# Folding the input product of a Fourier mixing layer on VectorE, with its gates opened first

## The reference

```
F_GROUPS, F_GROUP_DIM = 8, 128

def fourier_mix(u):
    ug = u.astype(jnp.float32).reshape(B, S, F_GROUPS, F_GROUP_DIM)
    y = jnp.fft.fft2(ug, axes=(1, 3), norm='ortho').real
    return y.reshape(B, S, F_WIDTH).astype(u.dtype)

def token_mix(h, w_in, w_fourier, w_ret, w_out):
    proj = h @ w_in
    u_f, q, k, v, g, a_f, a_r = jnp.split(proj, offsets, axis=-1)
    y_f = fourier_mix(u_f) @ w_fourier
    y_r = retention_branch(q, k, v, g) @ w_ret
    merged = jax.nn.sigmoid(a_f) * y_f + jax.nn.sigmoid(a_r) * y_r
    return merged @ w_out

h = rmsnorm_2(x, norm1_g[l]) * (1.0 + sc1) + sh1
x = x + g1 * token_mix(h, ...)
```

## Time and profile before

| | us |
|---|---|
| median of 3 runs | 2947.02 |
| lowest, highest | 2945.31, 2947.09 |
| the profiled execution, own time | 2945.48 |
| its span, first to last instruction | 2943.6 |

### The profile page before, as it was taken

How to read it: one execution, slowest core, us unless ns; L and a number is a source line. 1 busy time by engine, 2 the same in 40 slices (tenths; PEclk the granted TensorE clock), 3 DMA queues, 4 the chain that set the end, 5 groups by cost and what they waited for, 6 DMA issues and landing times.

```text
span 2943.6 us, 49397 instructions
## 1 busy us (share of the span) xinstructions
PE 2927.3 (99%) x19714; PEld 2451.0 (83%) x19714; DVE 1533.1 (52%) x2181; ACT 1105.5 (38%) x1663; POOL 1559.3 (53%) x1910
## 2 busy tenths in 40 slices
PE   9999999999999999999999999999999999999998
PEld 7877777788888888988888898888988888888887
DVE  5467787424556666753334274435542432473635
ACT  4454434333443332443433243323433342342323
POOL 6432233356546676546444556565465445575654
PEclk9999999999999999999999999999999999999999
DMA  5211111233326777423222223232233222223232
GB/s 172 92 45 41 42 54 57 93 143 101 122 97 221 253 273 252 148 79 128 85 92 72 93 87 115 86 107 85 94 108 115 78 77 94 93 94 99 95 100 72
DMA packets 92005, 320.50 MB, mean 109 GB/s; under 512 B 10112, under 2 KB 14336, under 8 KB 91520
## 3 DMA queue, kind: packets, MB, share of 16 engines
q1 hardware_dynamic: 84256, 301.34, 30.8%
q10 hardware_dynamic: 7520, 15.99, 1.6%
HBM read 313.36 MB, written 3.93 MB: 108 GB/s over the span
## 4 chain that ended last, share of the span: by engine, by line
PE 97%; issue 1%; POOL 1%; DMA 0%; DVE 0%; ACT 0%; SPq 0%; POOLq 0%; ACTq 0%; DVEq 0%
PE bank L826 26%; PE bank L830 25%; PE bank L827 25%; PE bank L1152 2%; PE bank L819 2%; PE bank L1163 2%; PE bank L820 2%; PE bank L821 2%; PE bank L1171 1%; POOL w_lo L757 1%; PE bank L858 1%; PE bank L857 1%; PE bank L856 1%; PE bank L1678 1%; PE bank L1677 1%
## 5 line engine op out<-in xcount | busy, mean ns | idle before, releaser
L757 POOL TENSOR_TENSOR w_lo<-w_raw,w_hi 128x256 fp32r<-128x256 f32 x1800 | 1464.8, 847 | 1044.5 <-ACT w_hi L1750 1034.5
L826 PE MATMUL bank<-act,w_hi 128*128 128x512 f32 (+1 forms) x3592 | 1363.0, 379 | 2.1 <-POOL w_lo L757 1.5
L830 PE MATMUL bank<-act,w_lo 128*128 128x512 f32 (+1 forms) x3592 | 1342.0, 374 | 0.0
L827 PE MATMUL bank<-act,w_hi 128*128 128x512 f32 (+1 forms) x3592 | 1340.9, 373 | 0.0
L826 PEld LDWEIGHTS bank<-act,w_hi 128*128 128x128 f32 x3592 | 676.7, 188 | 128.1 <-issue 9.3
L830 PEld LDWEIGHTS bank<-act,w_lo 128*128 128x128 f32 x3592 | 676.4, 188 | 120.5
L827 PEld LDWEIGHTS bank<-act,w_hi 128*128 128x128 f32 x3592 | 677.1, 189 | 111.0
L1750 ACT CAST w_hi<-w_raw 128x1024 fp32r<-128x1024 f32 x452 | 471.3, 1049 | 340.5 <-DMA w_raw<-in_weights 160.7
L1758 ACT ACTIVATE arena<-bank 128x512 f32<-128x512 f32 (+1 forms) x177 | 104.4, 594 | 416.5 <-PE bank L830 399.9
L775 POOL TENSOR_TENSOR stats<-stats,exponent 128x8 f32<-128x8 f32 (+2 forms) x38 | 46.6, 1226 | 299.5 <-DVE stats L2742 150.0
L2428 DVE TENSOR_TENSOR act<-tmp,act 128x512 fp32r<-128x512 f32 (+1 forms) x140 | 122.1, 872 | 77.6 <-ACT act L1777 72.7
(11 more groups left out here) (327 smaller groups left out, 2814.0 us busy)
## 6 DMA issues: line engine op xcount, KB each, us to landing
w_raw<-in_weights SPq DMA_DIRECT2D x469, 512.0 KB, 3.4
arena<-in_ada SPq DMA_DIRECT2D x96, 512.0 KB, 4.8
arena<-in_strips ACTq DMA_DIRECT2D x8, 448.0 KB, 3.6
arena<-in_x ACTq DMA_DIRECT2D x1, 2048.0 KB, 10.4
y_scratch<-tmp ACTq DMA_DIRECT2D x7, 256.0 KB, 2.0
arena<-y_scratch ACTq DMA_DIRECT2D x1, 1792.0 KB, 7.9
arena<-in_x SPq DMA_DIRECT2D x3, 512.0 KB, 7.8
arena<-in_lora_w ACTq DMA_DIRECT2D x8, 128.0 KB, 2.2
```

The lines of the kernel that those rows point to most:

```text
L757: ins = nc.gpsimd.tensor_tensor(w_lo[:, k, cols], weights_of(u)[:, cols], w_hi[:, k, cols].bitcast(F32), ALU.subtract)
L826: nc.tensor.matmul(o, wh, xh, start=first, stop=False)
L827: nc.tensor.matmul(o, wh, xl, start=False, stop=False)
L830: mm = nc.tensor.matmul(o, wl, xh, start=False, stop=last)
```

## The change

It replaces step 2 and reorders step 3 in both layers.

- **The order.** The first three tiles, those of the opening, are now gate tiles, and gates 3 and 4 follow. Then come nine folded tiles (`folded_tile`): a middle one with 8 output rows, and an even and an odd one for each of four pairs of feature groups, each 24 matmuls of 258 or 256 columns. Gates 5, 6 and 7 and the transforms stand between them as the list `FOURIER_ORDER` says. The eight output tiles come behind, with gate 7 between the fourth and the fifth.
- **Tokens are folded before the product.** Within the second half of the opening, VectorE adds and subtracts the two halves of the tokens mirrored (`fold`, four instructions for each block), ScalarE rounds the folded block, and VectorE makes its low part (`folded_low`). The first half's normalised blocks stay in SBUF for that (`FIRST_HALF`), where before they went through PSUM.
- **Weights are folded too.** `input_sums(p)` makes sum and difference of two whole units (two instructions of 1024 columns), the first within the opening at the twelfth of its 16 steps, the others behind it. `output_sums` is the old `weight_sums`.
- **The transform** works on pairs of groups of 64 waves: `fourier_features` four times for each layer, `fourier_tokens` with three matmuls of 257 columns and two of 255 in place of eight of 63 to 128.
- **Gates** are stored in `MERGED` by ScalarE; VectorE joins the even and odd output in `tmp` and multiplies.

The core of the diff (`...` marks what is left out):

```diff
+FOURIER_ORDER = [("gate", j) for j in range(5)] + [("middle",), ("even", 0), ("odd", 0), ("even", 1), ("odd", 1), ("gate", 5),
+                                                   ("even", 2), ("odd", 2), ("even", 3), ("odd", 3), ("gate", 6), "out"]
+FOURIER_ORDER += [("out", j) for j in range(4)] + [("gate", 7)] + [("out", j) for j in range(4, 8)]
...
-        p.plain(f"fourier_in{l}", "w_in_2", l, 0, 8)
-        p.split(f"fourier{l}", "A2", 8, before)
-        p.gated(f"fourier_out{l}", ("w_in_2", l, 5120, "A1"), ("w_fourier_2", l, 0, "A2"), 8, parts=True)
+        p.fourier(l)
...
+            def folded_tile(l, what):
...
+                    if KT * l + k + 1 > seen["folded"]:
+                        pe.wait_ge(sem("nf_low"), KT * l + k + 1)
+                        seen["folded"] = KT * l + k + 1
...
                 opening_halves(f"fourier_in{l}", f"n1_{l}", f"n1_{l}" if l else "final")
...
+                for j in (3, 4):
+                    gate_tile(f"fourier_out{l}", f"n1_{l}", j)
+                folded_tile(l, "middle")
+                folded_tile(l, ("even", 0))
+                folded_tile(l, ("odd", 0))
+                folded_tile(l, ("even", 1))
+                fourier_features(0)
+                folded_tile(l, ("odd", 1))
+                gate_tile(f"fourier_out{l}", f"n1_{l}", 5)
+                fourier_features(1)
+                fourier_tokens(0)
...
                     do(V_.scalar_tensor_tensor(normalised_half(q0 + i), H[:, j, half_cols(h)], gain(j),
                                                half_inverse(h), ALU.mult, ALU.mult), "tmp_ready")
+                    beside(i)
                     lows(i)
+                    behind(i)
...
+                def fold(i):
+                    if i < KT:
+                        return
+                    dve.wait_ge(sem("high_done"), splits[f"n1_{l}"][0] + i + 1)
...
+                    do(V_.scalar_tensor_tensor(o[:, 1:W2], x[:, 1:W2], TWICE[:, j:j + 1], mirrored, ALU.add, ALU.add))
+                    do(V_.tensor_tensor(o[:, HALF_WAVES:S], x[:, 1:W2], mirrored, ALU.subtract))
+                    do(V_.tensor_scalar(o[:, 0:1], x[:, 0:1], shift, None, ALU.add))
+                    do(V_.tensor_scalar(o[:, W2:HALF_WAVES], y[:, 0:1], shift, None, ALU.add), "nf_ready")
...
+                def input_sums(p):
...
+                    for v in (u, u + 1):
+                        dve.wait_ge(sem(f"w_landed{v % RAWS}"), 16 * (v // RAWS + 1))
+                    sums_free(i)
...
+                    do(V_.tensor_tensor(W_SUMS[:, i % 2, :], x, y, ALU.add))
+                    do(V_.tensor_tensor(y, x, y, ALU.subtract), "w_summed")
...
+                def behind(i):
+
+                    if i > KT + 1:
+                        folded_low(i - KT - 2)
+                    if i == KT + 3:
+                        input_sums(0)
...
+                    split_halves("n1_0", "final", lambda j: None, lambda j: both_gains[:, j:j + 1], shifts_of(0, 0),
+                                 lambda i: fold(i - 1), behind)
```

More of the change, by code:

```diff
@@ L1587, in cosines @@
[L1587 to L1594 removed]
+                    for what in ("middle", ("even", p), ("odd", p)):
+                        evacuated(pe, plan.folded[l][what])
@@ L1607, in fourier_tokens @@
[L1607 to L1612 removed]
+                    if n >= 2:
+                        pe.wait_ge(sem("f_low"), n - 1)
```

486 lines of the change are left out of this document (303 added, 183 removed).

## The result

| | before | after |
|---|---|---|
| median | 2947.06 us (4 runs, 2945.31 to 2947.33) | 2970.97 us (4 runs, 2969.84 to 2974.03) |
| profiled execution's span | 2943.6 us | 2968.8 us |

The ratio is 1.0084, 95% interval 1.0067 to 1.0102: **the change makes the kernel 24 us slower**. The forecast was 2953 us, slower, and the range ended at 2960. The direction was right. The size was a third of what came: the profiled execution was to take 7.5 us more than before and took 25.1 more.

What follows compares the result with a forecast made beforehand. TensorE, busy 99% of the span, was taken to bound the kernel, with VectorE pacing the opening's second half. 2945.5 us plus 4.8 (openings +30.5, first halves +0.6, behind -26.3) plus 3 for the clock gave 2953 us; range 2946 to 2960.

Steps and rivals of the forecast that it cites:

- Whatever is put on VectorE in this half beyond that, TensorE waits for: Opening's second half: VectorE has 0.9 us to spare in layer 0, 1.6 in layer 1; more delays TensorE.
- VectorE's half, 25.4 us: Opening's second half: VectorE's work with folds, low parts and first sums takes 25.4 us where it was 8.9.
- TensorE leaves the opening 1.1 us later: End of the opening: TensorE finishes 1.1 us after VectorE's last low part, at 1268.3 in layer 0.
- +15.9 and +15.2: Opening's end in layers 0 and 1: 15.6 and 14.9 us later from the second half, plus 0.3 each from the first.
- The clock, +3 once: Openings: TensorE's clock falls to 1.2 GHz, costing 3 us an opening (0 to 5), even chances each, likeliest once.
- The transform over the features keeps its columns: Feature transform behind the opening: columns unchanged, so no added TensorE time was counted for it.
- New waits of 2.2 us behind the opening: Behind the opening, each layer: queues for weights and output tiles add 2.2 us of TensorE waits, between 0 and 4.5.
- Nothing behind the output tiles: Retention behind the last output tile, both layers: change forecast at 0.
- Rival 3: Weights' queue behind the opening binds harder: 4.5 us waits, 2 more at the join, +4.3 a layer, 2959 to 2962; chance 0.09.
- the sum (+7.8 with the clock): Whole kernel: openings +30.5, first halves +0.6, behind them -26.3, giving +4.8 us, and +3 for the clock.
- That holds: Opening's first weight sums: the second unit is loaded 3.4 us after about 1246, before VectorE comes at 1251.5.

Runs made afterwards that it cites:

- the last run: Against the 2936.11 us kernel that folds behind the opening: first weight sums one fold later, folded block 5 rounded before gate 4's copy; 2932.51 us (0.9955).
- the late fold: Against the changed kernel: all token folding moved behind the opening, second half kept in SBUF, three gates before the folded tiles; 2960.57 us (1.0048).

## Why the prediction was right in sign and wrong in size

1. **"Whatever is put on VectorE in this half beyond that, TensorE waits for"**: right. It is why the change is slower, and the two runs without the fold show it.
2. **VectorE's half, 25.4 us**: 26.1. The terms were good; the one-column instructions were sized from a row of 0.20 and took 0.25, and 14 of them stand in it: 0.7 us, the whole difference.
3. **"TensorE leaves the opening 1.1 us later"**: it left 2.47 after the last low part, since its last two steps ran at 0.21 us a matmul. Here the clock's price stands, 1.4 us for an opening (the run with the clock kept up bounds it by the same 1.4), not the 3 of the separate term. With the first half's 0.4 the openings came to +18.1 and +17.5 in place of +15.9 and +15.2.
4. **The clock, +3 once**: the fall was rightly read from the earlier trace rows, in both openings instead of one. The price was too high: I took 2 us of the gates behind the opening to be lost, and in the profiled execution the clock was up again in the opening's last matmuls. In the three later profiles of the same opening it was low for 1.5 us behind layer 0's, so an execution can pay some 2.5 us for an opening.
5. **"The transform over the features keeps its columns"**: the step that failed most. It kept its columns, but its six matmuls alternate between 128 and 8 rows, and 10 records in 16 cost 0.20 to 0.21 instead of 0.11 (the expectation above counted 9): 0.9 us a pair, 3.6 a layer. Grouping took back 0.4 a pair, equal rows 0.66. The tokens took 2.37 where 2.24 was forecast, since one of the five matmuls has one row (there four starts lie 0.31 to 0.32 apart, the others 0.22; no run took it out), the last small transform 1.5 instead of 1.35, and each folded tile 2.96 instead of 2.88.
6. **New waits of 2.2 us behind the opening**: 3.9, of which 3.2 at the output tiles. The forecast compared TensorE's 3.0 with GpSimd's 3.3 us a unit and called it 1.7; the ring of cast, sums, join and copy was slower than GpSimd. That a ring through three engines sets a pace can't be seen from any one engine's price.
7. **Nothing behind the output tiles**: the retention began later, by 2.7 and 1.0 us. Rival 3 had 2 us a layer for that, at a chance of 0.09. VectorE's first rotary instruction (it turns queries and keys by a table) waits for that table's load, which ScalarE's queue starts behind its casts; in the kernel before and in the changed one:

```profile
1380.48 0.69 DVE L3276 TENSOR_TENSOR arena<-bank,table 128x512 f32<-128x512 f32 x1 [14.31 <-DMA arena<-in_rotary]
...
1394.58 0.69 DVE L3456 TENSOR_TENSOR arena<-bank,table 128x512 f32<-128x512 f32 x1 [16.84 <-DMA arena<-in_rotary]
```

From the last output tile's end that is 16.6 and 19.3 us, the same 2.7 (in layer 1 16.8 and 17.7). The casts behind it come late, GpSimd's low part behind them, and the value tile waits 2.42 us for that. Why the load came later no run shows.

Of the 17.7 us between the sum (+7.8 with the clock) and the trace (+25.5), items 5 and 6 with the tiles are 12.5, item 7 is 3.7, and the openings 4.5, less the 3 counted for the clock. The terms of this account are readings of single executions; the runs confirm the features (about 4 of 7 us) and the ring (2.6 of 6), and the folded tiles' 0.08 us each and item 7 were only read.

Rival 3 was the nearest in what it named (the weights' queue), and the run without the fold shows that queue exactly where the forecast had written "That holds". It held, because VectorE was late.

## What to carry to other kernels

When work is to be halved by preparing its operands, ask first when the preparing engine has to deliver. Here 17 us of VectorE cost 18 in the opening, where TensorE has nothing else to do, and in the last run 2 or 3 us of waits a layer behind three gates. Before counting a small matmul by its columns, look whether its weight tile has the shape of its neighbours'. And a wait that is hidden by slow work is still there: in the run without the fold and in the one with ScalarE's order changed again, VectorE came sooner to the weight sums and stood idle for the weights' transfer, 3.9 and 2.7 us.

## What the runs showed of the hardware

- Records of 130 columns started 0.11 us apart while the weight tile kept its shape, and 0.20 at a change between 128 and 8 rows or 128 and 1 columns; behind a change to a tile of 128 columns the second record came 0.21 later too. Sixteen times the rows at equal shape were cheaper than 8 (1.99 against 2.65 us a pair).
- TensorE's clock fell in a hole of 4.4 us behind a stretch in which it was busy 2.67 of 5.00 us, stayed at 1.2 GHz through 12.9 us in which it was busy 9.99, and came back to 2.4 GHz. With the sums moved out there was no such hole, and it fell all the same. In the late fold a fall stood before dense work and cost about 3.8 us.
- A VectorE instruction of one column took 0.21 us and 0.25 from start to start, against 0.46 for one with 255 columns.
